# Four groups of projections with the weights held in the array and all 256 tokens moved, so that they come out turned

## The reference

```python
def rms_norm(x, g):
    y = x * lax.rsqrt(jnp.mean(x * x, axis=-1, keepdims=True) + EPS)
    return y * g

# first block
h = rms_norm(x, norm_g[0])
q, k, v, g, lr, u_f, u_h, u_s = split(h @ w_in)      # q and k have 256 channels each
...                                                  # four mixers (gla, fnet, hyena, short convolution)
x = x + mix @ w_out
x = x + cross_attention(rms_norm(x, norm_g[1]), rms_norm(mem, mem_norm_g), w_xq, w_xkv, w_xo)
x = x + swiglu(rms_norm(x, norm_g[2]), w_gate_up, w_down)    # d_ff = 5632

def cross_attention(h, mem_n, w_q, w_kv, w_o):       # 4 heads of 512 channels
    q = h @ w_q;  k, v = split(mem_n @ w_kv)
    p = softmax(q @ k.T * 512 ** -0.5)
    return (p @ v) @ w_o

def swiglu(h, w_gate_up, w_down):
    gate, up = split(h @ w_gate_up)
    return (silu(gate) * up) @ w_down
# second block: a gated convolution layer and a differential attention layer
```

## Time and profile before

| | |
|---|---|
| median of three runs | 2384.68 us (2382.59 to 2384.91) |
| the profiled execution | 2382.62 us, span 2380.8 us |
| TensorE matmuls (PE) | 2366.8 us busy (99%), 10794 |
| TensorE weight loads (PEld) | 1935.1 us (81%), 10794 |
| VectorE (DVE) | 1379.4 us (58%) |
| ScalarE (ACT) | 1112.9 us (47%) |
| GpSimd (POOL) | 320.8 us (13%) |
| DMA | 185 GB/s mean over the span |
| TensorE's granted clock | full in all 40 slices |

### The profile page before, as it was taken

The page is one execution under the profiler, slowest core; times in us unless marked ns, Lnnn a source line. Parts: engine busy times, 40 slices in busy tenths (PEclk is TensorE's granted clock), DMA queues, the critical chain, the costliest instruction groups (busy, mean ns, idle before and its releaser), DMA issues.

```text
span 2380.8 us, 26679 instructions
## 1 busy us (share of the span) xinstructions
PE 2366.8 (99%) x10794; PEld 1935.1 (81%) x10794; DVE 1379.4 (58%) x1835; ACT 1112.9 (47%) x1426; POOL 320.8 (13%) x256
## 2 busy tenths in 40 slices
PE   9999999999999999999999999999999999999999
PEld 6777778888888888888888888888888888877887
DVE  5676756544445554454454555669984565456554
ACT  6433646444334444443344444544556544444653
POOL 1111010000000000000000000049987000011100
PEclk9999999999999999999999999999999999999999
DMA  9575446565435655555555555555655555654454
GB/s 336 190 234 156 157 158 229 178 193 194 154 129 177 212 184 187 194 190 192 192 187 193 195 183 188 188 184 177 195 178 182 188 177 182 193 173 141 152 169 140
DMA packets 218188, 440.65 MB, mean 185 GB/s; under 512 B 9711, under 2 KB 9898, under 8 KB 217361
## 3 DMA queue, kind: packets, MB, share of 16 engines
q1 hardware_dynamic: 213328, 421.88, 53.7%
q0 software_dynamic: 4736, 17.06, 2.2%
HBM read 432.64 MB, written 2.10 MB: 183 GB/s over the span
## 4 chain that ended last, share of the span: by engine, by line
PE 95%; DVE 2%; ACT 1%; DMA 1%; issue 0%; SPq 0%; POOL 0%; DVEq 0%; ACTq 0%; POOLq 0%
PE ps L96 93%; PE ps L99 3%; DMA RAW<-in_w_in 1%; DVE WLO L108 1%; ACT WHI L102 1%; SPq L134 0%; DVE ST L119 0%; DVE Alo L116 0%; POOL ST L108 0%; DVE ED L108 0%; DVE ND L116 0%; ACT WIN L102 0%; ACT BB L102 0%; ACT Ahi L102 0%; ACT L102 0%
## 5 line engine op out<-in xcount | busy, mean ns | idle before, releaser
L108 DVE TENSOR_TENSOR WLO<-RAW,WHI 128x1024 fp32r<-128x1024 f32 x701 | 854.8, 1223 | 757.5 <-ACT WHI L102 753.1
L102 ACT ACTIVATE WHI<-RAW 128x1024 fp32r<-128x1024 f32 x793 | 837.8, 1059 | 898.8 <-PE ps L96 892.5
L96 PE MATMUL ps<-WHI,Ahi 128*128 128x512 f32 x1904 | 754.1, 396 | 2.4 <-DVE Alo L116 2.0
L96 PE MATMUL ps<-WHI,Alo 128*128 128x512 f32 x1904 | 741.3, 390 | 0.0
L96 PE MATMUL ps<-WLO,Ahi 128*128 128x512 f32 x1904 | 740.8, 389 | 0.0
L96 PEld LDWEIGHTS ps<-WHI,Ahi 128*128 128x128 f32 x1904 | 357.6, 188 | 83.2 <-issue 6.3
L96 PEld LDWEIGHTS ps<-WHI,Alo 128*128 128x128 f32 x1904 | 357.4, 188 | 75.2
L96 PEld LDWEIGHTS ps<-WLO,Ahi 128*128 128x128 f32 x1904 | 357.7, 188 | 74.7 <-issue 2.9
L113 POOL TENSOR_SCALAR ST<-ST 128x1 f32<-128x1 f32 (+3 forms) x53 | 21.3, 401 | 1710.9 <-DVE ST L119 1441.1
L108 POOL TENSOR_TENSOR WLO<-RAW,WHI 128x1024 fp32r<-128x1024 f32 x92 | 218.9, 2405 | 54.6 <-ACT WHI L102 54.2
L116 DVE SCALAR_TENSOR_TENSOR ps<-YT,GC,ps 128x256 f32<-128x256 f32 x480 | 188.8, 485 | 8.0 <-ACT ps L102 8.0
(11 more groups left out here) (307 smaller groups left out, 2058.9 us busy)
## 6 DMA issues: line engine op xcount, KB each, us to landing
RAW<-in_w_gate_up SPq DMA_DIRECT2D x88, 1024.0 KB, 5.0
RAW<-in_a_w_in SPq DMA_DIRECT2D x48, 1024.0 KB, 5.1
RAW<-in_w_down SPq DMA_DIRECT2D x44, 1024.0 KB, 5.0
RAW<-in_w_in SPq DMA_DIRECT2D x39, 1024.0 KB, 6.4
RAW<-in_w_xkv SPq DMA_DIRECT2D x32, 1024.0 KB, 5.4
RAW<-in_w_kv SPq DMA_DIRECT2D x32, 1024.0 KB, 5.4
RAW<-in_b_w_in SPq DMA_DIRECT2D x32, 1024.0 KB, 5.3
RAW<-in_w_out SPq DMA_DIRECT2D x16, 1024.0 KB, 5.0
```

What stands on the lines that cost most here:

```text
L96: return self.e.matmul(o, l, r, start=start, stop=stop, skip_group_check=True)
L102: return self.e.activation(o, i, func, scale=scale, **kw)
L108: return self.e.tensor_tensor(o, a, b, op)
```

## The change

`qk`, `xkv` 0 to 3, `xq` 0 to 3, and all `gate` and `up` chunks (31 chunks) are laid as `lr` is: four blocks of 128 output channels are held, and 256 tokens are moved. The result lies turned, two blocks in each of the two banks. All their transposes, and the copies behind these, go. The norms are now multiplied in along the free axis from `RROW`, which is made three times (`x1`, `mem`, `x3`); the norm of the queries is not multiplied in but goes into the scale of the exponential. Buffers `QK` and `NT` go. VectorE evicts `qk`, `xkv` 0 to 3, `gate` and `up`; ScalarE evicts `xq` and does SiLU from SBUF to SBUF.

```diff
-        plan(("xkv", i), "act", "w_xkv", i * 512)
+        plan(("xkv", i), "dve" if i < 4 else "act", "w_xkv", i * 512)
+    def turned(name):
+        return name == "qk" or name[0] in ("xq", "gate", "up") or name[0] == "xkv" and name[1] < 4
-    put("lr", 0, ("qkT", 0), ("qkT", 1))
-    for i in range(4):
-        put(("xkv", i + 1), 0, ("xkT", i))
+    put_each(("xkv", 0), 2, [("rdiag", "mem"), ("rows", "mem")])
-        put(n, 0, ("qxT", h))
+    put_each(("gate", 0), 2, [("rdiag", "x3"), ("rows", "x3")])
     # TensorE
-            e.wait_ge(*of("qxT", 4 * h + 2))
-            e.wait_ge(*of("xkT", 14))
+            e.wait_ge(*evicted(("xq", h)))
+            e.wait_ge(*evicted(("xkv", 3)))
-            elif what == "ffT":
-                e.wait_ge(*evicted(("up", k)))
-                for q in (0, 2):
-                    turn(("ff", 4 * k + q), ("T_lo", "ff", 4 * k + q), lambda t, j: AC[:, t, (q + j) * P:(q + j + 1) * P])
+                    if turned(name):
+                        for n in range(4):
+                            o, c4 = ps[n // 2][:, n % 2 * T:(n % 2 + 1) * T], slice(n * P, (n + 1) * P)
+                            e.matmul(o, hi[:, j, c4], xhi[:, kk, :], k + j == 0 and n % 2 == 0, False)
+                            e.matmul(o, hi[:, j, c4], xlo[:, kk, :], False, False)
+                            i = e.matmul(o, lo[:, j, c4], xhi[:, kk, :], False, k + j == kt - 1)
+                        continue
     # ScalarE
             elif kind == "xq":
-                e.wait_ge(*of("pa", ("qxT", 4 * i - 2) if i else ("xkT", 14)))
-                evict_copy(name, lambda h: NT[:, h, :], scale=r2)
+                e.wait_ge(*full(name))
+                e.activation(QX[:, 4 * i:4 * i + 2, :], kc(psum(name)[0]))
+                e.activation(QX[:, 4 * i + 2:4 * i + 4, :], kc(psum(name)[1])).then_inc(*evict(name))
             elif kind == "gate":
-                e.wait_ge(*of("rstd", "x3"))
-                evict_copy(name, lambda h: GT[:, h, :], AF.Silu, r3)
+                e.wait_ge(*of("gate_scaled", i))
+                e.activation(GT[:, :, :], GT[:, :, :], AF.Silu).then_inc(*evict(name))
             elif what == "ffT":
-                    t_hi("ff", 4 * k + q, pa, "pa", ("ff", 4 * k + q))
+                e.wait_ge(*evicted(("up", k)))
+                for q in range(2):
+                    n = split_slot("ff", 4 * k + 2 * q)
+                    e.activation(Fhi[:, n:n + 2, :], kc(AC[:, q, :])).then_inc(*done("T_hi", "ff", 4 * k + 2 * q))
     # VectorE
+            elif kind == "qk":
+                e.stt(QT[:, :, :], kc(ps[0]), 0.125, row, AL.mult, AL.mult)
+                e.tensor_tensor(KT[:, :, :], kc(ps[1]), row, AL.mult).then_inc(*evict(name))
+            elif kind == "xkv" and i < 4:
+                e.tensor_tensor(XK[:, 4 * i:4 * i + 2, :], kc(ps[0]), row, AL.mult)
+                e.tensor_tensor(XK[:, 4 * i + 2:4 * i + 4, :], kc(ps[1]), row, AL.mult).then_inc(*evict(name))
+            elif kind == "gate":
+                for q in range(2):
+                    n = e.tensor_tensor(kc(GT[:, q, :]), kc(ps[q]), row, AL.mult)
+                n.then_inc(*done("gate_scaled", i))
             elif kind == "up":
-                e.stt(AC[:, 0, :], ps[0], r3[:, 0:1], GT[:, 0, :], AL.mult, AL.mult)
-                e.stt(AC[:, 1, :], ps[1], r3[:, 1:2], GT[:, 1, :], AL.mult, AL.mult).then_inc(*evict(name))
+                for q in range(2):
+                    e.tensor_tensor(kc(AC[:, q, :]), kc(ps[q]), row, AL.mult).then_inc(*done("up_scaled", i, q))
+                e.wait_ge(*evicted(("gate", i)))
+                e.wait_ge(*of("up_scaled", i, 1))
+                e.tensor_tensor(AC[:, :, :], AC[:, :, :], GT[:, :, :], AL.mult).then_inc(*evict(name))
-            elif what in ("xkT", "qxT"):
-                    e.tensor_copy((XK if what == "xkT" else QX)[:, q:q + 2, :], kc(pa.ap((what, q))[:, :])).then_inc(*done(what, q))
             elif what == "ffT":
-                    t_lo("ff", q, pa, ("ff", q))
+                    e.tensor_tensor(Flo[:, n:n + 2, :], kc(AC[:, q, :]), f(Fhi[:, n:n + 2, :]), AL.subtract) \
+                        .then_inc(*done("T_lo", "ff", 4 * k + 2 * q))
     # GpSimd, after x2's norm: r2x = norm x 512 ** -0.5, which the exponential takes as its scale
```

More of the change, by code:

```diff
@@ L468, in build_program @@
     put("sch", 7, ("back", 1, 0))
-    put_each("qk", 0, [("back", 1, 1), ("norm", 2), ("rdiag",), ("rows",)])
+    put_each("qk", 0, [("back", 1, 1), ("norm", 2), ("rdiag", "x1"), ("rows", "x1")])
     put("qk", 2, ("normed", 2))
     put_each("qk", 6, [("norm", 3), ("normed", 3)])
-    put("lr", 0, ("qkT", 0), ("qkT", 1))
     gla_slots = [("v", j) for j in range(8)] + [("fnet", j) for j in range(8)] + in_turn(("mo", 0), ("mo", 1))
@@ L848, in step @@
                 back(*a)
[L849 to L852, removed]
             elif what == "rows":
-                b, free = pa.take(("rows",), ("rows", 0))
+                b, free = pa.take(("rows", k), ("rows", k))
                 e.wait_ge(*free)
-                e.wait_ge(*of("rows_diag", 0))
+                e.wait_ge(*of("rows_diag", k))
                 for t in range(2):
                     i = e.matmul(b[:, t * P:(t + 1) * P], ONE[:, :], RDIAG[:, t, :], True, True)
-                i.then_inc(*done("pa", ("rows",)))
+                i.then_inc(*done("pa", ("rows", k)))
             elif what == "gates":
@@ L1085, in evict_chunk @@
                 evict_copy(name, lambda h: U[:, h, :], scale=r1)
-            elif kind == "qk":
-                e.wait_ge(*of("normed", 3))
-                evict_copy(name, lambda h: QK[:, h, :], scale=r1)
             elif kind == "v":
@@ L1094, in evict_chunk @@
                 evict_squares(name, "x2", i)
-            elif kind == "xkv" and i < 4:
+            elif kind == "xkv" and i >= 4:
                 e.wait_ge(*of("rstd", "mem"))
-                if i:
-                    e.wait_ge(*of("pa", ("xkT", 4 * i - 2)))
-                evict_copy(name, lambda h: NT[:, h, :], scale=rm)
-            elif kind == "xkv":
                 e.wait_ge(*of("T_lo", "mem", 14))
@@ L1437, in evict_chunk @@
             ps = psum(name)
[L1438 removed]
+            r1, row = cols(("r", "x1"), 2), RROW[:, :].unsqueeze(1).to_broadcast([P, 2, T])
             if kind in ("hy0", "hy1", "hy2"):
@@ L1776, in step @@
             elif what == "rdiag":
-                r = cols(("r", "x1"), 2)
-                e.wait_ge(*of("pb", ("back", 1, 1)))
-                e.wait_ge(*of("rstd", "x1"))
-                e.wait_ge(*of("d_id", 0))
+                r = cols(("r", k), 2)
+                if k == "x1":
+                    e.wait_ge(*of("pb", ("back", 1, 1)))
+                    e.wait_ge(*of("d_id", 0))
+                else:
+                    e.wait_ge(*of("pb", ("glao",)))
+                    e.wait_ge(*of("pa", ("rows", "x1" if k == "mem" else "mem")))
+                e.wait_ge(*of("rstd", k))
                 e.tensor_scalar(RDIAG[:, 0, :], IDN[:, :], r[:, 0:1], AL.mult)
-                e.tensor_scalar(RDIAG[:, 1, :], IDN[:, :], r[:, 1:2], AL.mult).then_inc(*done("rows_diag", 0))
+                e.tensor_scalar(RDIAG[:, 1, :], IDN[:, :], r[:, 1:2], AL.mult).then_inc(*done("rows_diag", k))
             elif what == "gmin":
@@ L1822, in step @@
                 e.wait_ge(*now("att_step"))
-                e.tensor_scalar(mx, mx, -XSC, AL.mult).then_inc(*done("att_max", k))
+                e.wait_ge(*of("r2x", 0))
+                e.stt(mx, mx, -1.0, cols("r2x", 2), AL.mult, AL.mult).then_inc(*done("att_max", k))
                 e.wait_ge(*of("att_exp", k))
@@ L1959, in evict_chunk @@
                 add_rstd("x2")
+                e.wait_ge(*of("rstd", "x2"))
+                e.tensor_scalar(cols("r2x", 2), cols(("r", "x2"), 2), XSC, AL.mult).then_inc(*done("r2x", 0))
             elif kind == "xo" and i == 3:
```

58 lines of the change are left out of this document (26 added, 32 removed).

## The result

| | before | after |
|---|---|---|
| median of the runs | 2383.69 us (4 runs) | 2406.74 us (3 runs, 2405.39 to 2406.78) |
| ratio to before | | 1.0095, 95% interval 1.0075 to 1.0114 |
| profiled execution, span | 2382.62, 2380.8 us | 2406.71, 2404.9 us |

A fourth execution of the changed kernel took 4247 us at a mean granted clock of 0.72 and is left out. The change makes the kernel slower by 23 us; the forecast was 16.7 us faster, with a range that ended at 2390. Rival 2 had named 2407.

The account below looks back on a forecast made before the run. TensorE's matmul count times their distance was taken as the bound. Terms -18.1 (transposes gone), +0.9 (more `rows` steps) and +0.5 (matmul pace) gave -16.7 us, from 2384.68 to 2368.0 us, range 2361 to 2390.

Parts of the forecast that it names:

- Rival 2: Changed chunks: weight loading disturbs the fp32r stream, 120 ns a matmul, +40 us, 2407 us; deciding from 116.2 ns; chance 13%.
- What bounds the kernel: Whole kernel: time is the number of TensorE matmuls times their distance; other engines matter only if TensorE waits.
- The pace of the new matmuls: Changed chunks: 5952 matmuls of 256 columns at 113.3 to 113.5 ns replace 2976 of 512; +0.5 us.
- both ends: Bounds on the price of the new matmuls' pace: 0 at 113.3 ns, +40 us at 120 ns.
- two to one: Old gate chunk at 226.5 ns (512 columns) against `lr` at 113.4 (256), taken as evidence against a loading disturbance.
- The turns: Transposes at 20 places in the old layout, 0.905 us each on TensorE's path, would go: -18.1 us.
- The two `rows`: Two more `rows` steps on TensorE, 0.46 us each, their waits covered: +0.9 us.
- Evictions at 0: New VectorE and ScalarE work at the ends of `gate` and `up` chunks stays hidden: 0 us.
- slack of 5.9 us: At chunk ends, spare time before TensorE wants the queued weight part; new operations ahead take at most 3.8 us.
- rival 3: Evictions at the ends of changed chunks make TensorE wait, 1 us at each of 31: 2399 us; chance 5%.
- Rival 1: Changed chunks: load no longer fits wholly or a fixed cost shows, 114.3 to 117 ns, +6 to +22 us; chance 16%.
- Rival 4: Restarts after small steps are shorter in the new layout, so more is gained: 2362 to 2365 us; chance 4%.

Follow-up runs that it names:

- experiment 2: Kernel before plus unread stretches of fp32 and bf16 matmuls behind its last product: 256-column fp32 passes 215.8 ns, bf16 215.8 (512 columns), 109.2 (256), 55.8 (128).
- experiment 4: Kernel before plus unread fp32r stretches with held and moved operands at other places, offsets or rows: 113.3 to 122.7 ns for 256 moved at varied offsets.
- experiment 1: Kernel before plus 14 unread stretches of 48 fp32r matmuls, columns moved and held varied: 226.67, 173.35, 146.67, 120.0 ns for 512, 384, 320, 256 moved, 128 held.
- the map: Shifted-token kernel with leads (small matmuls put ahead) of differing widths at almost every chunk from `gate` 0 to `up` 5, and some others: 2386.53 us, one run.

## Why the prediction was wrong

**What bounds the kernel: right.** All went by the number of matmuls and their distance; no engine made TensorE wait in the new kernel.

**The pace of the new matmuls: wrong, and alone enough.** This is the term of +0.5 us, which measured +39.7. I had both ends right, 0 and +40 us, and chose the wrong one. The reason given was that the earlier trace rows stand at two to one with a factor of four in loaded columns, so that a disturbance would need a fixed cost "of just the right size" to be hidden. The size was just right: the extra is 13.3 ns with 128 held for 256, 320, 384 and 512 columns moved, and 6.7 with 32 held and 256 moved. In numbers, 106.7 + 6.7 and 213.3 + 13.3 are two to one by coincidence. The row that was missing is one of 256 moved with 128 held in fp32r, and no row of before had it. I had put and the earlier trace rows in its place, which are fp32 at half the stream rate; experiment 2 shows that these don't see the disturbance.

**Rival 2: right in its price, its place and its threshold.** 120 ns, 2407 us, decided from 116.2 ns on: the mean distance over the 31 chunks was 118.0 ns in the kernels with shifted tokens, 116.0 with three leads and 115.3 in the last, and their ratios to the kernel before were 1.0045 and 1.005, 0.9998 and 0.9983. It was wrong in its form: the extra isn't linear in the columns held. And its cause, the load, isn't shown: no run has an fp32r matmul without a load of its own. That the pace also hangs on where the held operand begins (experiment 4) only points to it.

**The turns, -18.1: right.** Before, a `gate` chunk with a turn took 22.69 or 22.65 us and one without 21.76, so 0.93 or 0.89; after, all take 23.04. **The two `rows`, +0.9: right**; twelve records of `ps<-RDIAG,ONE` are there, and TensorE waits for none of them. **Evictions at 0: right.** The slack of 5.9 us was enough, and `WLO` is waited for 0.6 us in all, so rival 3 fell. **Rival 1** named two things. Its load that just doesn't fit fell: the load's own pace is 111.7 ns, below every one seen in the kernel. Its fixed cost for each matmul is the form that experiment 1 showed with 128 held, but with 120.0 ns outside its 114.3 to 117. (By its own sum, 2367.5 + 6, its range began at 2373.5 us and not at 2371.) **Rival 4** was right in its sign, with 0.5 us.

**The 1.6 us in `hy0`** are of a stretch at the lower granted clock, which the kernel before can have too, and have no part in the loss: from `qk` on the ledger gives 39.7 - 18.1 + 0.9 - 0.5 = 22.0 us, and 21.9 were measured.

What stays open: why 4-byte numbers at full rate lose 6.7 to 13.3 ns and more for each matmul, and what carries the pattern from one matmul to the next. The runs show only that it depends on where both operands begin, and on what came before. To leave `qk` and `xkv` 0 to 3 in the old layout, which by the ledger would save 5 x (1.28 - 0.9) = 1.9 us and the 0.45 us of one step `rows`, wasn't tried.

## What to carry to other kernels

When TensorE is the bound, a change of layout that keeps the columns moved but doubles the matmuls must be priced at the distance of exactly the new form, type, moved and held columns together; where the trace has no such row, give the costly end as much chance as the cheap one, and don't let a neat ratio of two rows decide. With fp32r and operands in place, 512 columns a matmul is the cheaper form: 226.7 ns against 2 x 120.0. And two chunks with the same instructions at two paces are a sign of placement: try the moved operand 16 bytes on, and look for a good pace that stays once it is reached. Measure both ways, since with 512 moved the same 16 bytes cost 5 ns, and expect little: the best kernel here is 0.17% faster than the one before, with leads found by trial.

## What the runs showed of the hardware

- An fp32r matmul costs its columns over 2.4 GHz and 13.3 ns more with 128 columns held (226.67, 173.35, 146.67, 120.0 ns for 512, 384, 320, 256), but in the best placing of 256 only 6.7 (113.3). bf16 and the fp32 pass of 256 columns cost 2.5 ns.
- The pace of a stretch of 256-column matmuls was one of 113.3, 116.7, 118.7 or 120.0 ns with the addresses unchanged, and one matmul ahead of it could change which (4 of 17 leads in the map set 113.3, and one kept it).
- In a stretch, fp32r matmuls with 128 columns held came no closer than 111.7 ns in the mean (128 and 192 moved alike), and 128 moved over 64 held came every 60.0 ns, so this is the pace of the load; bf16 matmuls with 128 held came every 55.8 ns.
- At the lower clock level, 1.2 GHz, the extra of fp32r is gone: matmuls of 512 columns over all 128 rows came every 426.7 ns, in `hy0` of the kernel after and behind the stretch below, which is 512 over 1.2 GHz and nothing more.
- The granted clock fell within both stretches of experiment 4 that used only 32 rows of the array, each behind one with 64 rows that still had the full clock, and the distance went from 227 to 427 ns. A window over the 32 matmuls of 512 columns:

```profile
2420.86:2432.42 11.56, 11.56 (x33) 0.62 0.00 0
```
